# The doubling inverse of a gated DeltaNet layer: the transposed inverse taken from transpositions instead of from products of its own

## The reference, cut to what matters

```python
low = jnp.where(strict, jnp.einsum('nbhid,nbhjd->nbhij', kb, k) * decay, 0.0)
a_mat = low + jnp.eye(C, dtype=f32)
rhs = jnp.concatenate([v * beta[..., None], kb * jnp.exp(gc)[..., None]], -1)
sol = lax.linalg.triangular_solve(a_mat, rhs, left_side=True, lower=True, unit_diagonal=True)
u, w = sol[..., :dv], sol[..., dv:]
```

## Time and profile before

| what | value |
|---|---|
| median of 3 runs | 1618.15 us (1612.44 to 1619.58) |
| profiled execution, its own time | 1617.51 us |
| its span, first to last instruction | 1615.7 us |
| mean granted PE clock | 0.978 of full |
| PE busy | 1504.4 us (93%) |
| DVE busy | 929.6 us (58%) |
| ACT busy | 599.0 us (37%) |
| head after head, start of the first T add | 133.14, 186.50, 239.85, 293.22 us |

### The profile page before, as it was taken

One profiled execution on the slowest core, in us unless ns is written; L12 is line 12 of the kernel. 1 busy time (PEld: TensorE's weight loads), 2 busy tenths in 40 slices (PEclk: granted clock), 3 DMA queues, 4 the chain that ended last, 5 costly groups with the idle time before them and its releaser, 6 DMA issues.

```text
span 1615.7 us, 21116 instructions
## 1 busy us (share of the span) xinstructions
PE 1504.4 (93%) x7549; PEld 1224.9 (76%) x7549; DVE 929.6 (58%) x1319; ACT 599.0 (37%) x897; POOL 173.4 (11%) x149
## 2 busy tenths in 40 slices
PE   6899999999889699999999899999896999999997
PEld 5778878887677678888788686665576888887886
DVE  5555665566555466666522625889875666665225
ACT  3542344234412244444312234454522444444210
POOL 3302220122102000000000201111101000000002
PEclk8999999999999899999999999999998999999999
DMA  5211111111120133333332221112121233333331
GB/s 161 52 40 40 39 39 39 39 39 42 37 64 15 53 104 99 96 91 105 129 104 92 66 78 40 53 34 70 52 66 52 79 96 99 91 104 121 102 103 66
DMA packets 156509, 116.73 MB, mean 72 GB/s; under 512 B 5738, under 2 KB 145452, under 8 KB 156460
## 3 DMA queue, kind: packets, MB, share of 16 engines
q1 hardware_dynamic: 156460, 116.06, 23.9%
HBM read 113.94 MB, written 2.10 MB: 72 GB/s over the span
## 4 chain that ended last, share of the span: by engine, by line
PE 79%; DVE 12%; issue 3%; ACT 3%; DMA 1%; SPq 1%; DVEq 0%; ACTq 0%
PE bank L1417 14%; PE bank L1419 14%; PE bank L1418 13%; PE bank L1405 7%; PE bank L1407 7%; PE bank L1406 7%; PE bank L1480 5%; PE bank L1473 4%; PE bank L1752 2%; DVE w_lo L322 1%; ACT w_hi L317 1%; SPq L388 1%; DVE x_tok L1136 1%; DVE bn L1140 1%; PE bank L1435 1%
## 5 line engine op out<-in xcount | busy, mean ns | idle before, releaser
L1417 PE MATMUL bank<-x_hi,w_hi 128*128 128x512 f32 (+1 forms) x1160 | 462.8, 399 | 28.9 <-DVE x_lo L896 25.5
L1419 PE MATMUL bank<-x_hi,w_lo 128*128 128x512 f32 (+1 forms) x1160 | 442.4, 381 | 0.0
L1418 PE MATMUL bank<-x_lo,w_hi 128*128 128x512 f32 (+1 forms) x1160 | 441.5, 381 | 0.0
L322 DVE TENSOR_TENSOR w_lo<-raw,w_hi 128x1024 fp32r<-128x1024 f32 x196 | 244.2, 1249 | 319.2 <-ACT w_hi L317 306.7
L1417 PEld LDWEIGHTS bank<-x_hi,w_hi 128*128 128x128 f32 x1160 | 223.0, 192 | 68.7 <-DVE w_lo L322 23.9
L317 ACT ACTIVATE w_hi<-raw 128x1024 fp32r<-128x1024 f32 x188 | 196.8, 1050 | 192.0 <-PE bank L1407 151.7
L1419 PEld LDWEIGHTS bank<-x_hi,w_lo 128*128 128x128 f32 x1160 | 222.2, 192 | 41.5
L1418 PEld LDWEIGHTS bank<-x_lo,w_hi 128*128 128x128 f32 x1160 | 223.0, 192 | 37.6 <-issue 3.6
L1405 PE MATMUL bank<-w_hi,u_hi 128*128 128x512 f32 x416 | 166.0, 399 | 17.5 <-issue 11.5
L1407 PE MATMUL bank<-w_hi,u_lo 128*128 128x512 f32 x416 | 163.4, 393 | 0.0
L1406 PE MATMUL bank<-w_lo,u_hi 128*128 128x512 f32 x416 | 163.2, 392 | 0.0
(11 more groups left out here) (262 smaller groups left out, 2042.3 us busy)
## 6 DMA issues: line engine op xcount, KB each, us to landing
raw<-in_ffn_w_up SPq DMA_DIRECT2D x88, 512.0 KB, 3.8
raw<-in_ffn_w_down SPq DMA_DIRECT2D x44, 512.0 KB, 3.3
raw<-in_gdn_w_in SPq DMA_DIRECT2D x32, 512.0 KB, 4.1
raw<-in_diff_w_in SPq DMA_DIRECT2D x24, 512.0 KB, 3.7
raw<-in_gdn_w_out SPq DMA_DIRECT2D x8, 512.0 KB, 3.3
raw<-in_diff_w_out SPq DMA_DIRECT2D x8, 512.0 KB, 3.3
x_tok<-in_x SPq DMA_DIRECT2D x4, 512.0 KB, 5.7
out_x<-x_tok SPq DMA_DIRECT2D x3, 512.0 KB, 2.7
```

The lines of the kernel that those rows point to most:

```text
L322: nc.vector.tensor_tensor(w_lo[:, s, :], raw[:, (base + r) % RAW, :], w_hi[:, s, :].bitcast(F32), ALU.subtract).then_inc(lo_ready, 1)
L1417: nc.tensor.matmul(out, hi, x_hi[:, k, cols], start=(k == 0), stop=False)
L1418: nc.tensor.matmul(out, hi, x_lo[:, k, cols], start=False, stop=False)
L1419: ins = nc.tensor.matmul(out, lo, x_hi[:, k, cols], start=False, stop=last)
```

## The change

For the five levels s = 2 to 32, `part(2, ...)` is taken out. Instead, at the start of each level from s = 4 on, directly behind the four products TM by LT, PE transposes the four matrices TM into bank X(e,2), and DVE copies the second half of each block's columns (128x256 in all, what `part(2, ...)` fed before) from there to TT. The copy stands on DVE's queue at the head of `added(i)`, behind `masked(i)` and what is between them, and is waited for by PE where the TT of the level before was waited for already. Level 64 keeps its product, its DVE add, and now is the only one that has them.

```diff
-LV = [f"{k}{s}" for s in LEVELS for k in ("P", "T", "TT") if (k, s) != ("T", LEVELS[-1])]
+LV = [key for i, s in enumerate(LEVELS)
+      for key in [f"P{s}"] + ([f"TT{LEVELS[i - 1]}"] if i else []) + [f"T{s}" if i < len(LEVELS) - 1 else f"TT{s}"]]
@@ VectorE
                 def added(i):
-
                     s = LEVELS[i]
+                    if i > 0:
+                        pe(f"TT{LEVELS[i - 1]}")
+                        new = halves(TT[e][:, :, :].rearrange("p n t -> p (n t)"), LEVELS[i - 1], 1)
+                        nc.vector.tensor_copy(new, halves(X(e, 2)[:, :], LEVELS[i - 1], 1)).then_inc(d_dve, 1)
                     if i < len(LEVELS) - 1:
                         pe(f"T{s}")
                         old = halves(TM[e][:, :, :].rearrange("p n t -> p (n t)"), s, 0)
                         nc.vector.tensor_tensor(old, halves(X(e, 1)[:, :], s, 0), old, ALU.add).then_inc(d_dve, 1)
-                    pe(f"TT{s}")
-                    old = halves(TT[e][:, :, :].rearrange("p n t -> p (n t)"), s, 1)
-                    nc.vector.tensor_tensor(old, halves(X(e, 2)[:, :], s, 1), old, ALU.add).then_inc(d_dve, 1)
+                    else:
+                        pe(f"TT{s}")
+                        old = halves(TT[e][:, :, :].rearrange("p n t -> p (n t)"), s, 1)
+                        nc.vector.tensor_tensor(old, halves(X(e, 2)[:, :], s, 1), old, ALU.add).then_inc(d_dve, 1)
@@ TensorE
                     four(0, at(LT), at(TM))
+                    if i > 0:
+                        four(2, at(TM), None, turn=True)
                     n_fill = 3 if i == 0 else 2
                     fill(p, p + n_fill)
@@ TensorE
                     if s != LEVELS[-1]:
                         part(1, TT, PB, s, 0)
-                    part(2, PB, TT, s, 1)
+                    else:
+                        part(2, PB, TT, s, 1)
```

## The result

| | before | after |
|---|---|---|
| median of 17 runs each | 1619.39 us | 1624.47 us |
| lowest to highest | 1612.44 to 1621.26 | 1622.26 to 1626.72 |
| profiled execution, its span | 1615.7 us | 1621.1 us |
| PE busy | 1504.4 us | 1497.0 us |
| DVE busy | 929.6 us | 928.5 us |

The ratio is 1.0035, with a 95% interval of 1.0026 to 1.0043. By the medians the changed kernel is 5.1 us slower, by the ratio 5.7 us, both within 0.5%. The forecast was +4.6 us on the profiled execution's time, so 1622.1 us; the changed kernel's profiled execution took 1622.87 us.

The account below looks back on a forecast made before the run. PE was taken to bound the DeltaNet stage. +0.6 us per head, +4.1 for seven heads, and +0.4 in the last gave +4.6 us on 1617.51 us: 1622.1 us, range 1613 to 1633.

Parts of the forecast that it names:

- What goes: part(2) of five levels, 0.89 us each: gain 0.16 us per level, but the full 0.89 behind the sum of squares.
- What comes on PE: Four transpositions in each of five levels: 0.44 us per group, not hidden, bounds 0.44 and 0.89.
- What comes on DVE: Copy 128x256 from a bank, 0.42 us; behind mask and tap at s = 4 and 8 it ends at 3.35.
- The lower bound, 0.29: Shortest time allowed for DVE's copy to TT, 0.29 us; it would take 1.8 us off the forecast.
- The last head: Without tap or sum of squares: s = 4 at 3.89 us, other four levels 4.35 each, 21.3 in all, +0.4.
- The sum: Levels from T add to T add: +0.6 us per head, +4.1 for seven heads, +4.6 in all.
- PE's passes decide: Rival: with T's wait hidden in the levels, 18 us faster, 1599.5 us; chance 0.05.
- DVE's queue more than counted: Rival: copy behind mask and tap at s = 4 and 8 costs more, +7 on the sum, 1629 us; chance 0.16.
- Transpositions as dear as products: Rival: PE's transposition groups cost what products cost, +18 us, 1640 us; chance 0.02.
- The clock: Rival: new PE gaps in each head lower the clock, +16 us, 1638 us; chance 0.05.
- the weight split's early start: DVE's split before s = 4 and s = 64 starts earlier, is over at 1.47 us, ahead of the mask.

## Why the prediction was right

- **What goes.** The removed products were priced at 0.16 us per level instead of 0.89. The run with only the removal shows 4.07 to 3.91, and the handover from T add to products is 0.48 us in the changed kernel, as forecast. Behind the sum of squares the whole 0.89 counted (4.93 to 4.03).
- **What comes on PE.** 0.44 us per group, taken from L1471, is what L1476 shows, and doubling the groups adds it again. The Trainium skill's 390 ns per transposition (VectorE: DVE Perf Modes, The three transpose paths), a figure for bf16, stands against four in 0.44 us here too; by that figure the sum would have been 45 us too high, by the prediction's estimate.
- **What comes on DVE.** The copy takes 0.41 to 0.42 us, as the add of the same width did. The lower bound, 0.29, was that of half the columns, and no row of a copy of this width was there. PE waits for it at s = 4 and 8 alone (0.38), as worked out from mask and tap. That the order was the cause, and not only stood beside it, the run with the copy ahead of the taps shows.
- **The last head.** At s = 4 without filler 3.95 us, not 3.89. The sum of 21.3 held.
- **The sum.** +4.6 us against +4.2 in the stage by the trace and +5.1 by the medians. The trace is the better witness: 1.2 us of the two spans' difference lie outside the stage, so that the medians come so close is in part luck.
- **The rivals.** PE's passes decide: excluded by the run with only the removal. DVE's queue more than counted: the place was right, the price not reached. Transpositions as dear as products: excluded. The clock: it stayed at 1.00 through all of the loop, with gaps of 0.65 us at four levels of each head, so in the loop it had no part in the result; but see below.
- **Not predicted.** The prediction called the weight split's early start harmless. In the changed kernel it was; with the filler split it was not, as it began 0.55 us before the end of POOL's L523. In the changed kernel it begins at 186.27, and POOL's last operation is over at 186.13.

## What to carry to other kernels

Work of the busiest engine can be the cover of its own wait. Before products are taken out, look at what the next instruction in line waits for and when that arrives: only the part beyond the arrival is a gain. When cheaper work takes the place of dear work, the order has to move with it: here the same substitution costs 5 us when left where the old one stood, and saves 12 to 14 with one filler step moved into the new gap and the copy put ahead of work that nobody waits for yet.

## What the runs showed of the hardware that was not expected

**The clock fell once on short gaps, though not in the loop.** In the run with only the removal, the last head's s = 4 has no filler, and the gaps between PE's products follow closely (0.52, 0.78, 0.52 us). Windows of 4 us (us, PE busy, PEld, DVE, ACT, POOL, granted clock):

```profile
444.00:448.00 4.00, 3.48 (x24) 3.06 (x22) 1.45 (x2) 1.73 (x2) 0.00 (x0) 1.00 0.12 47
448.00:452.00 4.00, 2.70 (x16) 2.33 (x15) 1.22 (x3) 0.55 (x1) 0.00 (x0) 0.72 0.42 131
452.00:456.00 4.00, 4.00 (x15) 3.42 (x14) 0.69 (x1) 0.51 (x1) 0.00 (x0) 0.50 0.00 0
456.00:460.00 4.00, 3.48 (x22) 3.09 (x22) 2.25 (x3) 0.00 (x0) 0.00 (x0) 0.93 0.15 25
```

The clock goes to 0.50, the level of 1.2 GHz, and level s = 8 takes 6.62 us instead of 3.91. In the changed kernel the like stretch left the clock at 1.00:

```profile
466.00:470.00 4.00, 2.71 (x23) 2.37 (x22) 1.74 (x4) 0.33 (x1) 0.00 (x0) 1.00 0.42 131
```

PE is busy for 2.70 us of 4 in both, and once the clock fell. These are two different kernels, so that alone does not show that it differs from execution to execution. The kernel with copy and filler moved and the one with the split moved too come nearer to that: their code is the same at the start of the last head, and in both PE waits there for 2.66 us for the same weight split. Two windows of the first, then the same two of the second:

```profile
440.00:444.00 4.00, 1.34 (x9) 0.93 (x8) 3.00 (x3) 1.67 (x2) 2.41 (x2) 1.00 0.00 0
444.00:448.00 4.00, 4.00 (x26) 3.52 (x25) 1.40 (x2) 1.02 (x1) 0.00 (x0) 1.00 0.78 236
...
440.00:444.00 4.00, 1.34 (x5) 0.93 (x4) 3.70 (x3) 0.92 (x1) 1.66 (x2) 0.84 0.09 10
444.00:448.00 4.00, 4.00 (x19) 3.40 (x18) 0.69 (x1) 1.06 (x1) 0.00 (x0) 0.73 0.73 255
```

Behind the same gap the clock stayed once and fell to 0.50 once. What decides it stays open; such a fall costs some 3 us where it was seen whole (6.62 against 3.91), and that belongs to the scatter of the runs. The Trainium skill (TensorE: Matmul & The Clock Gate, A second HAM failure mode) tells of a clock that swings through frequent short idle times; the last head agrees with it in that one run, the loop, with 0.65 us idle at four levels of each head and PE busy 94% of the time, does not.

**A weight split on DVE, two operands in SBUF, is held by the POOL operation that runs when it begins.** The same weight split takes 1.22 us when POOL rests and 1.63 when it begins during POOL's L523. It ends at 183.37, 1.08 us after L523 has ended. The kernel before has the same in each head, at another of its weight splits:

```profile
181.41 1.29 POOL L537 TENSOR_TENSOR TT<-TT,ident 128x512 f32<-128x512 f32 x1
...
182.20 1.59 DVE L322 TENSOR_TENSOR w_lo<-raw,w_hi 128x1024 fp32r<-128x1024 f32 x1
...
182.66 2.04 POOL L520 TENSOR_TENSOR GU<-upto,gdec 128x512 f32<-128x512 f32 x1
```

Here it ends 1.09 us after L537 has ended, though POOL's next operation runs beside all the rest of it. In the first seven heads of the kernel before and of the one with copy and filler moved every such split that begins during a POOL operation ends 1.07 to 1.09 us behind that operation's end, whatever its own length (1.58 to 1.91), and every other one takes 1.22 or 1.23. So the rows read as if it were held until that operation ends, and not run slower beside it. Operations that read a bank kept their 0.68 and 0.42 us beside POOL (in the kernel before, a mask at 183.71 beside L520 and the T add at 186.50 beside L522). The Trainium skill (GPSIMD Engine Reference, Specifications) says that GpSimd's SBUF interfaces are shared with VectorE, with contention for DVE instructions of two SBUF inputs; the rows agree.
